# Turning the input rows of a hybrid decoder trunk by a product with a diagonal, and the first weight chunks tile by tile

## The reference

```python
h = jnp.concatenate([meta, x], axis=1)          # 16 + 256 rows of 2048
u = rmsnorm(h, pre_mix_g[i])                    # x / sqrt(mean(x^2) + eps) * g
proj = u @ w_in[i]                              # 2048 x 4608
q, k, v, u_pool, u_conv = jnp.split(proj, splits, axis=-1)
# stick-breaking attention, causal pooling and a Conformer convolution,
# joined by an output projection; then rmsnorm, a SwiGLU FFN and the residual
```

## Time and profile before

| | |
|---|---|
| median of 3 runs | 1150.9 us (1150.71 to 1151.04) |
| the profiled execution | 1150.66 us, its span 1148.7 us |
| TensorE busy | 1132.2 us, 99% |
| VectorE, ScalarE, GpSimd busy | 59%, 46%, 3% |
| mean granted TensorE clock | 0.998 |
| first product of the projection | 18.23 us |

### The profile page before, as it was taken

How to read it: one execution, slowest core, us unless ns; L and a number is a source line. 1 busy time by engine, 2 the same in 40 slices (tenths; PEclk the granted TensorE clock), 3 DMA queues, 4 the chain that set the end, 5 groups by cost and what they waited for, 6 DMA issues and landing times.

```text
span 1148.7 us, 21345 instructions
## 1 busy us (share of the span) xinstructions
PE 1132.2 (99%) x8383; PEld 1075.2 (94%) x8383; DVE 672.1 (59%) x787; ACT 527.7 (46%) x642; POOL 32.2 (3%) x45
## 2 busy tenths in 40 slices
PE   9999999999999989999999999999999999999996
PEld 8999999999999989999999999999999888888885
DVE  5599985545556875555556555655565544444543
ACT  6644465755555563433433343334333434343431
POOL 2000101000000220000000000000000000000000
PEclk9999999999999999999999999999999999999999
DMA  7555544434455366665666666565656555555552
GB/s 248 173 168 172 175 129 147 137 115 136 130 181 179 99 200 185 184 186 181 191 188 183 181 184 183 182 187 181 194 172 197 186 199 188 199 188 196 189 195 91
DMA packets 173647, 200.39 MB, mean 174 GB/s; under 512 B 6257, under 2 KB 149825, under 8 KB 173201
## 3 DMA queue, kind: packets, MB, share of 16 engines
q1 hardware_dynamic: 172848, 197.30, 54.7%
q0 software_dynamic: 608, 1.41, 0.4%
q10 hardware_dynamic: 144, 1.05, 0.3%
HBM read 197.63 MB, written 2.10 MB: 174 GB/s over the span
## 4 chain that ended last, share of the span: by engine, by line
PE 96%; DVE 2%; ACT 0%; issue 0%; POOL 0%; POOLq 0%; DVEq 0%; ACTq 0%
PE ps L960 23%; PE ps L962 23%; PE ps L963 23%; PE ps L1280 7%; PE ps L1279 7%; PE ps L1278 7%; PE ps L991 1%; PE ps L1086 1%; PE ps L1074 1%; DVE u L762 1%; DVE arena L875 1%; PE ps L1103 1%; PE ps L1154 1%; DVE xT L882 0%; PE ps L1011 0%
## 5 line engine op out<-in xcount | busy, mean ns | idle before, releaser
L691 DVE TENSOR_TENSOR w_lo<-raw,w_hi 128x1024 fp32r<-128x1024 f32 x368 | 451.8, 1230 | 427.8 <-ACT w_hi L419 427.4
L419 ACT ACTIVATE w_hi<-raw 128x1024 fp32r<-128x1024 f32 x368 | 389.0, 1058 | 500.8 <-PE ps L963 367.2
L960 PE MATMUL ps<-u,w_hi 128*128 128x256 f32 (+1 forms) x1984 | 566.3, 285 | 2.1 <-DVE u L762 1.4
L962 PE MATMUL ps<-u,w_hi 128*128 128x256 f32 (+1 forms) x1984 | 560.6, 283 | 0.0
L963 PE MATMUL ps<-u,w_lo 128*128 128x256 f32 (+1 forms) x1984 | 558.9, 282 | 0.0
L960 PEld LDWEIGHTS ps<-u,w_hi 128*128 128x128 f32 x1984 | 374.1, 189 | 3.3 <-DVE u L762 1.2
L963 PEld LDWEIGHTS ps<-u,w_lo 128*128 128x128 f32 x1984 | 374.4, 189 | 0.0
L962 PEld LDWEIGHTS ps<-u,w_hi 128*128 128x128 f32 x1984 | 373.8, 188 | 0.2
L1278 PE MATMUL ps<-w_hi,ffn 128*128 128x512 f32 x352 | 136.9, 389 | 0.0
L1279 PE MATMUL ps<-w_lo,ffn 128*128 128x512 f32 x352 | 136.9, 389 | 0.0
L1280 PE MATMUL ps<-w_hi,ffn 128*128 128x512 f32 x352 | 136.9, 389 | 0.0
(11 more groups left out here) (167 smaller groups left out, 535.2 us busy)
## 6 DMA issues: line engine op xcount, KB each, us to landing
raw<-in_w_gate SPq DMA_DIRECT2D x88, 512.0 KB, 4.3
raw<-in_w_up SPq DMA_DIRECT2D x88, 512.0 KB, 3.5
raw<-in_w_down SPq DMA_DIRECT2D x88, 512.0 KB, 3.6
raw<-in_w_in SPq DMA_DIRECT2D x72, 512.0 KB, 3.5
raw<-in_w_out SPq DMA_DIRECT2D x32, 512.0 KB, 3.3
arena<-in_x SPq DMA_DIRECT2D x2, 1024.0 KB, 6.1
out<-f_acc SPq DMA_DIRECT2D x3, 512.0 KB, 2.8
side<-in_w_pw POOLq DMA_DIRECT2D x1, 1024.0 KB, 10.8
```

The lines of the kernel that those rows point to most:

```text
L419: act.activation(w_hi[:, slot, :], raw[:, slot, :], ACT.Copy).then_inc(hi_done, 1)
L691: dve.tensor_tensor(w_lo[:, slot, :], raw[:, slot, :], hi_view(w_hi[:, slot, :]), ALU.subtract).then_inc(lo_done, 1)
L960: pe.matmul(outs[m], w_hi[:, slot, at], x_hi, start=start and not (one_bank and m), stop=False, skip_group_check=True)
L962: pe.matmul(outs[m], w_hi[:, slot, at], x_lo, start=False, stop=False, skip_group_check=True)
```

## The change

The rows are no longer scaled and then transposed. For each of the three row tiles a diagonal matrix of the inverse norms is made (`diag_m`, `diag`), and the turning becomes a product of the unscaled rows (stationary) with this diagonal (moving), which transposes and scales in one. It is split into `turn_first` (meta rows and first row tile) and `turn_second` (second row tile). The second row tile is loaded in two halves, its squares are divided in other parts. The first weight chunk is split before the copies of tile 0, and chunk q+1 behind the copies of chunk q's tiles. In the first four chunks TensorE waits for the low part of each tile alone, multiplies it, and turns tile kt+4 behind it. The warm-ups are spread in another way (4, 4 and 10 instead of 10, 4 and 4).

```diff
-WARM_LOAD, WARM_ROWS, WARM_PARTS, WARM_FFN = 26, 10, 4, 30
+WARM_LOAD, WARM_ROWS, WARM_PARTS, WARM_START, WARM_FFN = 26, 4, 4, 10, 30
...
-            for m in range(NQ):
-                sp_eng.dma_start(xr[:, m, :], x[0, m * P:(m + 1) * P, :]).then_inc(x_landed[m], 16)
+            sp_eng.dma_start(xr[:, 0, :], x[0, 0:P, :]).then_inc(x_landed[0], 16)
+            for part, landed in ((slice(0, D // 2), x_half), (slice(D // 2, D), x_landed[1])):
+                sp_eng.dma_start(xr[:, 1, part], x[0, P:2 * P, part]).then_inc(landed, 16)
...
             inv_rms(r0[0:META, 2:3], ss0[0:META, 2:3], D, r0_done)
-            act.wait_ge(r0_done, 1)
-            act.activation(xsm[0:META], xr[0:META, 2, :], ACT.Copy, scale=r0[0:META, 2:3]).then_inc(xs_act, 1)
+            act.wait_ge(x_half, 16)
+            act.activation(xs[:, 1, 0:D // 2], xr[:, 1, 0:D // 2], ACT.Square, accum_out=ssp[:, 0:1]).then_inc(ss_act, 1)
+            act.wait_ge(ss_dve, 1)
+            inv_rms(r0[:, 0:1], ss0[:, 0:1], D, r0_done)
             act.wait_ge(x_landed[1], 16)
-            act.activation(xs[:, 1, 0:D // 2], xr[:, 1, 0:D // 2], ACT.Square, accum_out=ss0[:, 1:2]).then_inc(ss_act, 1)
+            act.activation(xs[:, 1, D // 2:3 * D // 4], xr[:, 1, D // 2:3 * D // 4], ACT.Square,
+                           accum_out=ssp[:, 1:2]).then_inc(ss_act, 1)
             act.wait_ge(ss_dve, 3)
-            inv_rms(r0[:, 0:2], ss0[:, 0:2], D, r0_done)
-            act.wait_ge(r0_done, 2)
-            act.activation(xs[:, 1, 0:D // 2], xr[:, 1, 0:D // 2], ACT.Copy, scale=r0[:, 1:2]).then_inc(xs_act, 1)
+            inv_rms(r0[:, 1:2], ss0[:, 1:2], D, r0_done)
...
+            split(0)
             for kt in range(KT):
...
-                if kt % CK == CK - 1:
-                    split(kt // CK)
+                if kt % CK == CK - 1 and kt < KT - 1:
+                    split(kt // CK + 1)
...
+            dve.wait_ge(r0_done, 1)
+            dve.tensor_scalar(diag_m[0:META], ident[0:META, 0:META], r0[0:META, 2:3], None, ALU.mult).then_inc(diag_done, 1)
+            dve.wait_ge(r0_done, 2)
+            dve.tensor_scalar(diag[:, 0, :], ident, r0[:, 0:1], None, ALU.mult).then_inc(diag_done, 1)
...
-            for m, n in ((0, 0), (0, 1), (1, 1)):
-                half = slice(n * D // 2, (n + 1) * D // 2)
-                dve.tensor_scalar(xs[:, m, half], xr[:, m, half], r0[:, m:m + 1], None, ALU.mult).then_inc(xs_dve, 1)
+            dve.tensor_scalar(diag[:, 1, :], ident, r0[:, 1:2], None, ALU.mult).then_inc(diag_done, 1)
+            split(0)
...
-            def turn_rows(kts):
-
-                for kt in kts:
...
-                    pe.transpose(ps[:, b, 0:META], xsm[0:META, cols], ident[0:META, 0:META])
-                    pe.transpose(ps[:, b, META:META + P], xs[:, 0, cols], ident)
-                    pe.transpose(ps[:, b, META + P:TOK], xs[:, 1, cols], ident).then_inc(u_made, 1)
-
-            turn_rows(range(0, CK))
+            def turn_first(kt):
+
+                if kt >= 4:
+                    pe.wait_ge(u_lo, kt - 3)
+                b, cols = 4 + kt % 4, slice(kt * P, (kt + 1) * P)
+                pe.matmul(ps[:, b, 0:META], xr[0:META, 2, cols], diag_m[0:META], start=True, stop=True)
+                pe.matmul(ps[:, b, META:META + P], xr[:, 0, cols], diag[:, 0, :], start=True, stop=True)
+
+            def turn_second(kt):
+                b, cols = 4 + kt % 4, slice(kt * P, (kt + 1) * P)
+                pe.matmul(ps[:, b, META + P:TOK], xr[:, 1, cols], diag[:, 1, :], start=True, stop=True).then_inc(u_made, 1)
+
+            pe.wait_ge(diag_done, 2)
+            for kt in range(CK):
+                turn_first(kt)
             keep_warm(WARM_PARTS)
+            pe.wait_ge(diag_done, 3)
+            for kt in range(CK):
+                turn_second(kt)
+            keep_warm(WARM_START)
 
             def early_work(q):
-                if q < CK - 1:
-                    turn_rows(range((q + 1) * CK, (q + 2) * CK))
-                    if q == 0:
-                        keep_warm(WARM_PARTS)
                 if q == VEC_AT:
                     pe.wait_ge(u_lo, KT)
...
                     early_work(q0 + s)
-                    pe.wait_ge(u_lo, (s + 1) * CK)
-                    products(q0 + s, s, range(s * CK, (s + 1) * CK), lambda kt: normed(kt, lo), outs,
-                             s == 0, s == CK - 1, one_bank)
+                    if q0 + s >= CK:
+                        products(q0 + s, s, range(s * CK, (s + 1) * CK), lambda kt: normed(kt, lo), outs,
+                                 s == 0, s == CK - 1, one_bank)
+                        continue
+                    for k in range(CK):
+                        kt = s * CK + k
+                        pe.wait_ge(u_lo, kt + 1)
+                        products(q0 + s, s, [kt], lambda kt: normed(kt, lo), outs, kt == 0, kt == KT - 1, one_bank,
+                                 at=k, used=k == CK - 1)
+                        if kt + CK < KT:
+                            turn_first(kt + CK)
+                            turn_second(kt + CK)
```

More of the change, by code:

```diff
@@ L175, in build_trunk @@
         r0, c = carve(cst, c, 3)
+        ssp, c = carve(cst, c, 4)
+        diag, c = carve(cst, c, 2, P)
+        diag_m, c = carve(cst, c, META)
         ssd, c = carve(cst, c, NQ, DN)
@@ L253, in build_trunk @@
             sem("const_step"), sem("const_ready"), sem("pads_ready"), sem("pads0"), sem("lg_done"))
-        ss_dve, ss_act, r0_done, xs_dve, xs_act = (
-            sem("ss_dve"), sem("ss_act"), sem("r0_done"), sem("xs_dve"), sem("xs_act"))
+        x_half, ss_dve, ss_act, r0_done, diag_done = (
+            sem("x_half"), sem("ss_dve"), sem("ss_act"), sem("r0_done"), sem("diag_done"))
         grow_turned, grow_done, vec_turned, vec_done, u_made, xt_made, xt_kept, u_hi, u_lo = (
@@ L700, in _ @@
                                      accum_out=ss0[:, 0:1]).then_inc(ss_dve, 1)
+            dve.wait_ge(const_ready, 1)
+            dve.wait_ge(r0_done, 1)
+            dve.tensor_scalar(diag_m[0:META], ident[0:META, 0:META], r0[0:META, 2:3], None, ALU.mult).then_inc(diag_done, 1)
+            dve.wait_ge(r0_done, 2)
+            dve.tensor_scalar(diag[:, 0, :], ident, r0[:, 0:1], None, ALU.mult).then_inc(diag_done, 1)
             dve.wait_ge(x_landed[1], 16)
-            dve.scalar_tensor_tensor(xs[:, 1, D // 2:D], xr[:, 1, D // 2:D], 1.0, xr[:, 1, D // 2:D], ALU.mult, ALU.mult,
-                                     accum_out=sst[:, 0:1]).then_inc(ss_dve, 1)
+            dve.scalar_tensor_tensor(xs[:, 1, 3 * D // 4:D], xr[:, 1, 3 * D // 4:D], 1.0, xr[:, 1, 3 * D // 4:D],
+                                     ALU.mult, ALU.mult, accum_out=ssp[:, 2:3]).then_inc(ss_dve, 1)
             dve.wait_ge(ss_dve, 2)
-            dve.wait_ge(ss_act, 2)
-            dve.tensor_tensor(ss0[:, 1:2], ss0[:, 1:2], sst[:, 0:1], ALU.add).then_inc(ss_dve, 1)
-            dve.wait_ge(r0_done, 2)
-            for m, n in ((0, 0), (0, 1), (1, 1)):
-                half = slice(n * D // 2, (n + 1) * D // 2)
-                dve.tensor_scalar(xs[:, m, half], xr[:, m, half], r0[:, m:m + 1], None, ALU.mult).then_inc(xs_dve, 1)
+            dve.wait_ge(ss_act, 3)
+            dve.tensor_reduce(ss0[:, 1:2], ssp[:, 0:3], AX.X, ALU.add).then_inc(ss_dve, 1)
+            dve.wait_ge(r0_done, 3)
+            dve.tensor_scalar(diag[:, 1, :], ident, r0[:, 1:2], None, ALU.mult).then_inc(diag_done, 1)
+            split(0)
             for kt in range(KT):
@@ L950, in _, with products @@
         def _(pe):
-            def products(q, slot, kts, rhs, outs, first, last, one_bank):
+            def products(q, slot, kts, rhs, outs, first, last, one_bank, at=0, used=True):
                 pe.wait_ge(lo_done, q + 1)
@@ L957, in products @@
                     for m in range(2):
-                        at = slice(k * BLK + m * P, k * BLK + (m + 1) * P)
+                        w = slice((at + k) * BLK + m * P, (at + k) * BLK + (m + 1) * P)
                         start = first and k == 0
-                        pe.matmul(outs[m], w_hi[:, slot, at], x_hi, start=start and not (one_bank and m), stop=False,
+                        pe.matmul(outs[m], w_hi[:, slot, w], x_hi, start=start and not (one_bank and m), stop=False,
                                   skip_group_check=True)
-                        pe.matmul(outs[m], w_hi[:, slot, at], x_lo, start=False, stop=False, skip_group_check=True)
-                        mm = pe.matmul(outs[m], w_lo[:, slot, at], x_hi, start=False,
+                        pe.matmul(outs[m], w_hi[:, slot, w], x_lo, start=False, stop=False, skip_group_check=True)
+                        mm = pe.matmul(outs[m], w_lo[:, slot, w], x_hi, start=False,
                                        stop=last and k == len(kts) - 1, skip_group_check=True)
-                mm.then_inc(chunks_used, 1)
+                if used:
+                    mm.then_inc(chunks_used, 1)
             def normed(kt, lo=0):
```

## The result

The changed kernel takes 1160.13 us (median of 6 runs, 1158.33 to 1160.42), the kernel before in the same series 1151.05 (1150.71 to 1152.27): a ratio of 1.0073, with a 95% interval of 1.0062 to 1.0084. The profiled execution took 1160.42 us with a span of 1158.4; that of before 1150.66 and 1148.7. The direction and the range of the prediction hold.

A forecast was written before the change was run, and what follows sets the result against it. TensorE's queue was taken to bound the kernel; turning 6.9 plus stall 1.3 less gains 0.1 and 0.2 made +7.9 us on the median 1150.9, so 1158.8 us, range 1154.8 to 1161.5.

The forecast's parts named there:

- What bounds it: Whole kernel: TensorE's queue bounds it, so a microsecond lost or saved before its steady stream is one of the whole.
- Input, norms, diagonals: Prologue: diagonals ready earlier than TensorE reaches them; only the wait before the first tile is gained, 0.1 us.
- The split of the first chunk: Prologue: first weight chunk's split moves before tile 0, covered by TensorE's warm-ups and turning; cost 0.
- The turning: 16 tiles in the prologue: fp32 products replace transposes, 0.96 us a tile instead of 0.53, 6.9 us in all.
- The stall: Before the vectors' transpose: tile 15 is turned right in front, so TensorE stands 1.3 us for its copy.
- The small gains: Prologue: 0.1 us from the first tile's wait, 0.2 us from faster first product passes behind turning products.
- The sum: Whole kernel: 6.9 + 1.3 - 0.1 - 0.2 = +7.9 us, giving 1158.8 us.
- rival 4: Turning: mode change worth four, +14.6, 1165.5 us; also a half-speed clock behind the 1.3 us stall; together chance 0.04.
- cheap loads: Turning: short passes and loads slip beside long ones, only two extra passes count; +4.5, 1155.4 us, chance 0.17.
- the gaps of transposing: Turning: 0.16 and 0.20 gaps belong to transposes and vanish in products; +1.2, 1152.1 us, chance 0.07.
- dear loads: Turning: each of the two 16-row passes waits for the other; +10.6, 1161.5 us, chance 0.10.
- the four to one: Turning: fp32 transposes four times faster than products; +14.6, 1165.5 us, chance 0.04 together with the clock.

The follow-up runs named there:

- Experiment 4: Changed kernel without the 14 warm-ups between the first turned parts, the second parts and the first product: 1157.89 us.
- experiment 1: Changed kernel with transposes in place of the three turning products, rows then not scaled: 1153.24 us.
- experiment 3: Changed kernel with only the 16-row turning product made a transpose, meta rows then not scaled: 1157.36 us.
- experiment 2: Changed kernel with the vectors' transposes in front of chunk 4 instead of chunk 3: 1158.01 us.
- experiment 7: Kernel before with first chunk split ahead of tile 0 and tile-by-tile multiplying and turning, by transposes of scaled rows: 1153.45 us, ratio 1.0015.
- experiments 5, 6 and 9: 2.2 us wait filled with 9 warm-up products: changed kernel 1158.72 us; kernel before 1150.79; changed kernel also with vectors' transposes later, 14 warm-ups removed 1154.95.
- experiment 8: Kernel before with tile-by-tile transposes, vectors' transposes in front of chunk 4, 6 warm-ups fewer, 2.2 us wait filled: 1149.93 us, ratio 0.9986.

## Why the prediction was right, point by point

- *What bounds it.* TensorE's queue does: 8.24 us of delay at 43 us are 8.24 us at 423 us, pass for pass.
- *Input, norms, diagonals.* The diagonals were done at 9.68 and 11.37 (reckoned: 9.8 and 11.9); TensorE began turning at 11.22 (reckoned 11.0) and took the second diagonal at 14.98 (14.8). It waited for neither, and the first product started at 18.02 (17.9). Experiment 4 shows that the input side had at least 2.4 us in hand. For a late landing of the gains I put 0 of "0 to 0.3". Their transpose came at 9.97 instead of 9.71, but not for that: TensorE didn't wait for them here, the first warm-ups ended that much later, because their change of pace (last section) came later. The same point moves between 4.1 and 7.1 us over the eleven profiles, so I take that part of the delay for chance and not for the change.
- *The split of the first chunk* took place from 11.14 to 13.46, beside TensorE's turning: cost 0, as said.
- *The turning.* 0.97 us for a tile (said: 0.96), 6.9 us in all (6.9), by experiment 1. For the 16-row product it was 0.16 (0.11 and 0.05 said, together 0.16), by experiment 3; the two parts of that were not measured singly. Two passes for each fp32 product, in 32 records for 16 calls of each line. The rule of four to one (the Trainium skill, page "TensorE: Matmul & The Clock Gate", Terms) doesn't hold for these shapes: it is two to one in passes.
- *The stall.* 1.24 us by experiment 2, 1.3 said; it is visible again, by itself, in experiment 7.
- *The small gains.* Of the -0.3 the first part holds: from the gains' transpose to the first turned tile it is 1.25 us with 8 warm-up passes where it was 2.71 with 20, and 12 passes of 0.112 are 1.34, so 0.12 was gained (said: 0.1). The other, -0.2 for a first product pass that would no longer be slow behind a product, was wrong. Behind each turned tile it still takes 0.21 (19.74 to 19.95), as it does behind warm-up products (18.02 to 18.23). The trace of before showed that already: its first product pass, at 18.23, stands behind warm-up products, and the next begins 0.21 later:

```profile
18.44 0.29 PE L962 MATMUL ps<-u,w_hi 128*128 128x272 f32 x1
```

- *The sum.* Said: 6.9 + 1.3 - 0.3 = 7.9. Measured: 6.90 by experiment 1 and 1.24 by experiment 2, 8.14, against 7.98 for the whole way, which leaves -0.16 for the small gains, 0.12 of it found. The stall came out 0.06 smaller than said and the small gains 0.14 smaller, so these two errors partly cancel. With the 0.26 at the start the mark is 8.24 late. With the wait filled in both kernels it is 7.9 between medians.
- *What failed* is one sentence under rival 4, that the clock "should hold" behind the 2.2 us wait since it did so in one profile. Going by the times, it falls there in 32 of 57 runs of the kernel before (one more, at 1151.48, lies between the groups) and in five of six of the changed one, for 1.4 to 1.8 us. I had a falling clock in view, but behind the new stall, and took one execution for all. The forecast also started from 1150.9, a median of three runs that were all of the lower group, and so was a forecast for the lower group, where the one run is at 1158.33, 0.5 below it; the median of six lies in the upper. It stayed inside the range because the range was wide, not because this was foreseen. The profiles of the two kernels differ by 8.24 + 1.52 = 9.76 us. Whether the changed kernel falls into it more often its six runs can't tell. In the series of experiments 1 to 4, though, 18 of the 23 runs of its four versions are of the upper group and 10 of 14 of the kernel before beside them, which is no clear difference. Why the clock falls in one execution and not in the next stays open.

The rivals: cheap loads (+4.5) and the gaps of transposing (+1.2) fall by experiments 1 and 3, dear loads (+10.6, 1.12 for a tile) by the 0.97, the four to one by the passes.

## What to carry to other kernels

The queue of an engine that bounds a kernel is a sum: where it has no waits, nothing that arrives earlier is a gain, and each operation that is put on it costs its full time, however idle the others are. Scaling inside a transposing product isn't free in fp32: here it took two passes instead of one, and 0.16 us more for a product that moves only 16 columns. When steps are made finer, look for the wait behind the last of them that the coarse order had covered; and before comparing two profiles to a microsecond, look at the spread of the runs and at the granted clock behind the longest wait of TensorE.

## What the runs showed of the hardware that I had not expected

- After one idle stretch of 2.2 us the granted clock goes to 1.2 GHz in some executions of one program and not in others, and costs 1.5 us when it does. Filling 2.0 of the 2.2 us with products of ones left no run in the upper group in the 24 of experiments 5, 6 and 9 and the 11 of experiment 8, and their four profiles show no drop there, at no cost to the sum that waits. The new stall in front of the vectors (1.1 us of idle time) showed no such drop in any profile.
- In the first microseconds the clock column says 1.00 while the passes say otherwise: the warm-up passes start 0.21 us apart and later 0.11, and the change of pace came between 4.1 and 7.1 us in the eleven profiles, at 6.5 in the kernel before and 7.1 in the changed one. At the very start the spacing of passes is to be read, not the column.
